# Two fused transformer blocks: the first block's head chain moved two weight blocks forward, function sets loaded by hand, and a normalisation moved into the heads loop

## The reference, cut to what matters

```
f = sigmoid(hf);  g = lb + (1 - lb) * f;  log_g = log(g);  kk = 1 - g
q = silu(hq) * 128 ** -0.5
o = hgrn2_scan(q, kk, hi, log_g)          # decays exp(sums of log_g), pair products, masks
o = rms_norm(o, hg_norm_w) * silu(hg)     # then 16 attention heads, branches, projections
...
uv = gelu(uv); u, v = split(uv)
v = (v - mean(v)) * rsqrt(var(v) + 1e-5) * ln_g + ln_b      # over 1024 channels
y_a = u * (einsum(w_s, v) + b_s)
```

## Time and profile before

| | |
|---|---|
| median of 3 runs | 2972.29 us (2972.26 to 2983.88) |
| profiled execution | 2973.5 us, span of the instructions 2971.7 us |
| PE busy | 2883.4 us, 97% of the span |
| DVE busy | 2171.6 us, 73% |
| ACT busy | 1504.5 us, 51% |
| mean granted TensorE clock | 0.992 |

### The profile page before, as it was taken

How to read it: one execution, slowest core, us unless ns; L and a number is a source line. 1 busy time by engine, 2 the same in 40 slices (tenths; PEclk the granted TensorE clock), 3 DMA queues, 4 the chain that set the end, 5 groups by cost and what they waited for, 6 DMA issues and landing times.

```text
span 2971.7 us, 42894 instructions
## 1 busy us (share of the span) xinstructions
PE 2883.4 (97%) x16334; PEld 2470.7 (83%) x16334; DVE 2171.6 (73%) x3307; ACT 1504.5 (51%) x2256; POOL 123.6 (4%) x121
## 2 busy tenths in 40 slices
PE   8999999999999999999998999999999999999997
PEld 6888888878888888888887888888888888888886
DVE  7777777778777777777786666667768887777775
ACT  5555555556554444444464445455555555555554
POOL 0000000000100000000050000000010000000001
PEclk9999999999999999999999999999999999999999
DMA  6444544445556556556654565555555655555563
GB/s 217 159 157 148 160 148 152 150 137 189 186 185 194 189 189 193 189 187 191 197 172 149 160 180 162 169 180 170 186 181 171 185 191 189 187 185 184 184 191 107
DMA packets 157023, 520.22 MB, mean 175 GB/s; under 512 B 28947, under 2 KB 31379, under 8 KB 156819
## 3 DMA queue, kind: packets, MB, share of 16 engines
q1 hardware_dynamic: 155376, 513.90, 54.2%
q10 hardware_dynamic: 1440, 3.59, 0.3%
HBM read 515.32 MB, written 2.10 MB: 174 GB/s over the span
## 4 chain that ended last, share of the span: by engine, by line
PE 72%; DVE 18%; ACT 6%; issue 4%; DMA 0%; SPq 0%; DVEq 0%; ACTq 0%; POOL 0%; POOLq 0%
PE acc L348 32%; PE acc L350 16%; DVE w_lo L1047 7%; PE psT L348 7%; PE psX L348 7%; ACT w_hi L664 4%; PE psT L350 3%; PE psX L350 3%; DVE work L1053 1%; DVE HS L1190 1%; DVE probs L1121 1%; ACT probs L714 1%; PE acc_first L348 1%; DVE soft L1122 1%; PE psS L476 1%
## 5 line engine op out<-in xcount | busy, mean ns | idle before, releaser
L1047 DVE TENSOR_TENSOR w_lo<-w_raw,w_hi 128x1024 fp32r<-128x1024 f32 (+1 forms) x960 | 1173.9, 1226 | 601.9 <-ACT w_hi L664 590.6
L664 ACT ACTIVATE w_hi<-w_raw 128x1024 fp32r<-128x1024 f32 (+1 forms) x960 | 1004.9, 1053 | 741.7 <-PE acc L350 554.8
L348 PE MATMUL acc<-XU,w_hi 128*128 128x512 f32 x3472 | 1239.1, 400 | 4.5 <-issue 3.9
L350 PE MATMUL acc<-XU,w_lo 128*128 128x256 f32 x3472 | 973.7, 280 | 0.0
L348 PEld LDWEIGHTS acc<-XU,w_hi 128*128 128x128 f32 x3472 | 655.2, 189 | 163.7 <-issue 7.5
L348 PE MATMUL acc<-XY,w_hi 128*128 128x512 f32 x2112 | 757.7, 402 | 13.7 <-DVE G L1053 4.6
L350 PEld LDWEIGHTS acc<-XU,w_lo 128*128 128x128 f32 x3472 | 658.1, 190 | 1.1
L350 PE MATMUL acc<-XY,w_lo 128*128 128x256 f32 x2112 | 592.5, 281 | 0.0
L348 PEld LDWEIGHTS acc<-XY,w_hi 128*128 128x128 f32 x2112 | 398.8, 189 | 118.4 <-issue 8.5
L350 PEld LDWEIGHTS acc<-XY,w_lo 128*128 128x128 f32 x2112 | 400.6, 190 | 0.1
L348 PE MATMUL psT<-XY,w_hi 128*128 128x512 f32 x632 | 225.6, 398 | 5.0 <-DVE w_lo L1047 4.5
(11 more groups left out here) (233 smaller groups left out, 2513.9 us busy)
## 6 DMA issues: line engine op xcount, KB each, us to landing
w_raw<-in_weights SPq DMA_DIRECT2D x956, 512.0 KB, 3.7
bias<-in_rel_bias SPq DMA_DIRECT2D x8, 384.0 KB, 5.6
bias<-in_rpb_back SPq DMA_DIRECT2D x32, 96.0 KB, 6.4
w_raw<-in_weights SPq DMA_DIRECT2D x8, 384.0 KB, 3.1
hT<-in_x_t SPq DMA_DIRECT2D x8, 256.0 KB, 6.1
out_dram<-G ACTq DMA_DIRECT2D x4, 512.0 KB, 3.1
G<-in_range_sums ACTq DMA_DIRECT2D x1, 576.0 KB, 4.6
G<-in_pair_masks ACTq DMA_DIRECT2D x1, 576.0 KB, 5.6
```

What stands on the lines that cost most here:

```text
L348: nc.tensor.matmul(bank[:, :], hi[:, k, col:col + P], X[:, k0 + k, :], start=first and k == 0, stop=False, skip_group_check=True)
L350: done = nc.tensor.matmul(bank[:, 0:T], lo[:, k, col:col + P], X[:, k0 + k, 0:T], start=False, stop=last and k == nk - 1, skip_group_check ...
L664: act.activation(w_hi[s][:, 0:n], w_raw[s][:, 0:n], ACT.Copy).then_inc(hi_done, 1)
L1047: V.tensor_tensor(w_lo[s][:, 0:n], w_raw[s][:, 0:n], w_hi[s][:, 0:n].bitcast(F32), ALU.subtract).then_inc(lo_ready, 1)
```

## The change

1. In `heads1` the tiles hf and hq change places (the weight stream too), and the chain from the sigmoid of hf to the last masks runs two block positions earlier: transposes at b = 5, decays at 6, 8, 10, 12, pair products at 8, 10, 12, 14. `tile_pairs` goes from 18 to 17, `scan_out` from 19 to 18, the head's norm from 21 to 20. The scores, the softmax and the gate tiles stay where they were.
2. Function sets are loaded by hand: the sigmoid set at b = 0, the one with Ln just before it at b = 3 and the sigmoid set again behind it, and at b = 5 a set that holds both Ln and Exp. The same set is loaded ahead of the norms and of the last phase, the sigmoid set ahead of the branches, Gelu and then Ln/Exp in `heads2`.
3. The two norms before `gmv` move behind its second block. The value sums go behind blocks 5, 7, ... 15 of `gmv` and 0 and 1 of `heads2`; centring, squares and their sums into blocks 2 to 6 of the first iteration of `heads2`. There the values are normalised at b = 7 instead of 0, and transposed and mixed behind blocks 7 and 8 instead of 4 and 6.
4. The 16 multiplications of `hT` (L1329) move from `gmv` to two per iteration of `heads2`.

```diff
             after1 = {
-                7: [transpose_pair(wk(0), "lg_ready", "lgT_full")],
-                8: [decays(0)],
+                5: [transpose_pair(wk(0), "lg_ready", "lgT_full")],
+                6: [decays(0)],
+                8: [pair_products(0), decays(1)],
                 9: [transpose_pair(wk(5), "vi_ready", "vT_full")],
-                10: [pair_products(0), decays(1)],
-                12: [pair_products(1), decays(2)],
+                10: [pair_products(1), decays(2)],
+                12: [pair_products(2), decays(3)],
                 13: [scores(0, P, 1)],
-                14: [pair_products(2), decays(3), transpose_pair(wk(5), "avz_ready", "avT_full", "v_ready")],
+                14: [pair_products(3), transpose_pair(wk(5), "avz_ready", "avT_full", "v_ready")],
                 15: [scores(1, T, 1)],
-                16: [pair_products(3)],
-                18: [tile_pairs],
-                19: [scan_out, prob_transposes(0, 1)],
-                20: [attend(0, 1), prob_transposes(1, 1)],
-                21: [scan_rms, attend(1, 1)],
+                17: [tile_pairs],
+                18: [scan_out],
+                19: [prob_transposes(0, 1)],
+                20: [scan_rms, attend(0, 1), prob_transposes(1, 1)],
+                21: [attend(1, 1)],
             }
...
+            first2 = after2 | {
+                0: [value_sums(value_sum, 6)],
+                1: [value_sums(value_sum, 7)],
+                4: [value_sums(value_square_sum, 0, 1, 2, 3)],
+                6: [value_sums(value_square_sum, 4, 5, 6, 7)],
+                7: [scores(0, T, 2), transpose_pair(wk(3), "vh_ready", "vh_full")],
+                8: [mix, transpose_pair(wk(5), "avz_ready2", "avT_full2")],
+            }
...
@@ ACT, heads1 @@
+                    if i and b == 0:
+                        act.preload_act_table(ACT.Sigmoid)
                     if b == (1 if i else 4):
+                        sigmoid_of(0, "hf_z", "hf_sig", i)
+                    if b == (3 if i else 4):
+                        act.wait_ge(S("g_ready"), i + 1)
                         sigmoid_of(2, "hq_z", "hq_sig", i)
-                    if b == (3 if i else 4):
-                        act.wait_ge(S("q_ready"), i + 1)
-                        sigmoid_of(0, "hf_z", "hf_sig", i)
+                        act.preload_act_table(ACT.Ln)
+                        act.activation(wk(0), wk(0), ACT.Ln).then_inc(S("lg_ready"), 1)
+                        act.preload_act_table(ACT.Sigmoid)
                     if b == 5:
-                        act.wait_ge(S("g_ready"), i + 1)
-                        sigmoid_of(3, "hg_z", "hg_sig", i)
-                        act.activation(wk(0), wk(0), ACT.Ln).then_inc(S("lg_ready"), 1)
-                    if b == 7:
                         act.wait_ge(S("lgT_full"), i + 1)
                         act.activation(lg_hi[:, :, :], psT[:, 0:T], ACT.Copy).then_inc(S("lg_hi_ready"), 1)
-                    if b in (8, 10, 12, 14):
-                        k = (b - 8) // 2
+                        act.wait_ge(S("q_ready"), i + 1)
+                        sigmoid_of(3, "hg_z", "hg_sig", i)
+                        act.preload_act_table_set(LOG_EXP)
+                    if b in (6, 8, 10, 12):
+                        k = (b - 6) // 2
...
@@ DVE, first iteration of heads2 @@
+                    if b == (0 if i else 7):
+                        if i == 0:
+                            dve.wait_ge(S("gv_rstd"), 1)
+                        normalized_values(i)
+                    if i == 0 and b == 2:
+                        dve.wait_ge(S("gv_sum"), 1)
+                        link(V.tensor_scalar(wk(8), psT[:, 0:T], 1.0 / WIDTH, None, ALU.mult))
+                    if i == 0 and 2 <= b < 6:
+                        center(2 * b - 4)
+                        center(2 * b - 3)
+                    if b == (6 if i else 9):
+                        mixed_values(i)
```

More of the change, by code:

```diff
@@ L579, in _, with value_sum, value_square_sum @@
             ffn("ffn1last", 0, XY, XU, S("act1_ready"))
+            def value_sum(t):
+                pe.wait_ge(S("gv_ready"), t + 1)
+                done = nc.tensor.matmul(psT[:, 0:T], ones[:, :], G[:, 24 + t, :], start=t == 0, stop=t == HEADS - 1)
+                if t == HEADS - 1:
+                    done.then_inc(S("gv_sum"), 1)
+            def value_square_sum(t):
+                pe.wait_ge(S("gv_sq"), t + 1)
+                nc.tensor.matmul(psE[:, 0:T], ones[:, :], value_squares[t % 4], start=t == 0, stop=t == HEADS - 1)\
+                  .then_inc(S("gv_sq_used"), 1)
             p = ph["gmv"]
@@ L592, in _ @@
                     rms_sum(1, psX)
[L593 to L601, removed]
+                if b % 2 and b >= 5:
+                    value_sum((b - 5) // 2)
             def mix(i):
+                if i == 0:
+                    pe.wait_ge(S("ws_in"), 16)
                 pe.wait_ge(S("vn_ready"), i + 1)
@@ L609, in mix, with value_sums, job @@
                 done.then_inc(S("mix_full"), 1)
+            def value_sums(which, *tiles):
+                def job(i):
+                    for t in tiles:
+                        which(t)
+                return job
             after2 = {
@@ L668, in copy_cross @@
                 act.wait_ge(w_used, p.block(i, b) + 1)
-                act.activation(cross[:, c % 2, :], bank[:, T:2 * T], ACT.Copy).then_inc(cross_ready, 1)
+                act.activation(cross[:, p.cross(i, c) % 2, :], bank[:, T:2 * T], ACT.Copy).then_inc(cross_ready, 1)
             def rstd(dst, src, width, eps, tmp, done):
@@ L884, in _ @@
                         copy_cross(p, i, t, b, acc[t % 2])
+                    if b == 0:
+                        act.preload_act_table(ACT.Gelu_apprx_tanh)
                     if b == 1:
@@ L948, in ffn2 @@
                     tile += s.half if s.kind == "up" else (2 if s.group < 0 else 1)
+            act.preload_act_table(ACT.Silu)
             ffn2("ffn2first", 0)
@@ L1052, in tile_sum @@
                 dve.wait_ge(cross_ready, p.cross(i, c) + 1 - RAW // 2)
-                mark(V.tensor_tensor(dst, bank[:, 0:T], cross[:, c % 2, :], ALU.add), acc_free,
+                mark(V.tensor_tensor(dst, bank[:, 0:T], cross[:, p.cross(i, c) % 2, :], ALU.add), acc_free,
                      p.tile(i, t) + 1 + TILE_CREDIT)
@@ L1191, in _ @@
                              S("qE_ready"), i * 4 + k + 1)
-                    if b == 9:
-                        scaled_tile(p, i, 4, b, 4, bank, wk(7), S("k_z"), i + 1)
-                    if b in (10, 12, 14, 16):
-                        k = (b - 10) // 2
+                    if b == 6:
+                        dve.wait_ge(S("hg_sig"), i + 1)
+                        if i == 0:
+                            dve.wait_ge(S("hgw_in"), 16)
+                        link(V.scalar_tensor_tensor(wk(3), wk(3), hgw, wk(4), ALU.mult, ALU.mult))
+                    if b == 7:
+                        scaled_tile(p, i, 3, b, 3, bank, wk(5), S("vi_ready"), i + 1)
+                    if b in (8, 10, 12, 14):
+                        k = (b - 8) // 2
                         a, h = divmod(k, 2)
@@ L1208, in _ @@
                                 link(ins)
+                    if b == 9:
+                        scaled_tile(p, i, 4, b, 4, bank, wk(7), S("k_z"), i + 1)
+                        dve.wait_ge(S("bias1_in"), 16 * i + 16)
+                        link(V.memset(bias[0:64, :, P:P + 64], MASKED))
                     if b == 11:
@@ new lines, in normalized_values, with mixed_values @@
+            def normalized_values(i):
+                link(V.tensor_tensor(work[:, 3:4, 0:T], G[:, ds(i + 24, 1), :], rsv.rearrange("p (a t) -> p a t", a=1), ALU.mult))
+                mark(V.tensor_scalar(wk(3), wk(3), cols[:, ds(i + C_LNG, 1)], cols[:, ds(i + C_LNB, 1)], ALU.mult, ALU.add),
+                     S("vh_ready"), i + 1)
+            def mixed_values(i):
+                dve.wait_ge(S("mix_full"), i + 1)
+                if i == 0:
+                    dve.wait_ge(S("bs_in"), 32)
+                bs = HS[:, 2:4, :, :].rearrange("p a b c -> p (a b) c")[:, ds(i, 1), :].to_broadcast([P, NT, P])
+                link(V.tensor_tensor(wk(1).rearrange("p (a t) -> p a t", a=NT), psA[:, 0:T].rearrange("p (a t) -> p a t", a=NT),
+                                     bs, ALU.add))
+                dve.wait_ge(S("u_ready"), i + 1)
+                mark(V.tensor_tensor(wk(1), wk(1), wk(0), ALU.mult), S("ya_z2"), i + 1)
+                dve.wait_ge(S("yah_ready2"), i + 1)
+                mark(V.tensor_tensor(XU[:, ds(i, 1), T:2 * T], work[:, 1:2, 0:T],
+                                     XU[:, ds(i, 1), 0:T].bitcast(F32), ALU.subtract), S("ya_ready2"), i + 1)
@@ L1467, in weight_block @@
         t = b // 2
-        starts = [0, 1, 3, 2, 5, 4, 6]
+        starts = [1, 0, 3, 2, 5, 4, 6]
         col = starts[t] * WIDTH + i * P if t < 7 else (7 * WIDTH + (t - 7) // 2 * D + (t - 7) % 2 * P + i * (2 * P))
```

157 lines of the change are left out of this document (77 added, 80 removed).

## The result

| | before | changed |
|---|---|---|
| median, fresh runs (18 each) | 2981.78 us (2970.38 to 2999.74) | 2992.20 us (2981.36 to 3004.71) |
| ratio, 95% interval | | 1.0035 (1.0019 to 1.0051) |
| profiled execution | 2973.5 us, clock 0.992 | 3000.5 us, clock 0.990 |

The change costs 10.4 us (5.7 to 15.2), where +0.4 was forecast.

What follows compares the result with a forecast made beforehand. PE, busy 97% of the span, was taken as the bound, so only its idle time, slow clock or added work counts. The terms summed to +0.4 on 2972.3, rounded 2973 us, own range 2962 to 2984 (chance 0.60).

Steps and rivals of the forecast that it cites:

- `tile_pairs`: First heads: PE's eight waits for DVE's mask products go, -21.6 us.
- `lg_lo` and the transposes ahead of it: First decay in the heads: PE's wait for the logarithm's low part grows from 1.05 to 3.4 us, +18.1 in sum.
- `scan_out`: First heads: a new wait for ACT's copy `AT`, 1.5 us eight times, +12.0 us.
- slow clock in the heads: Slow clock behind all seven `lg_lo` waits of 3.4, none behind those of 1.5: 10.5 instead of 6.0, +4.5 us.
- start of `branch1`: End of the heads: `branch1` waits about 0.6 instead of 3.07 us, without slow clock, -4.0 us.
- `gmv` and `heads2`: Third tile's wait and clock -5.4, sums between stages -7.6, new idles in the first iteration of `heads2` +5.7 us.
- last norm: End of the run: one load less on the path to the output, -1.3 us.
- rival (a): The wait at `scan_out` doesn't come: 12 us less, 2961 us; chance 0.13.
- the idles of 2.7 in the first iteration: First iteration of `heads2`: PE idle 2.3 us behind block 4 and 2.7 behind block 7.
- rival (b): `lg_lo` wait stays 1.05, no wait at `scan_out`, no slow clock in the heads: -40, 2932 us; chance 0.10.
- (d): Each function load in the `lg_lo` chain is followed by 1.38 us idle: 19 more, 2992 us; chance 0.02.
- Rival (c): Wait at `scan_out` is 2.6 us and slows the clock in every head: 21 more, 2994 us; chance 0.13.

Runs made afterwards that it cites:

- heads: Only the first heads' part of the change (chain two blocks forward, hand-loaded function sets, tiles, branch start) put into the kernel before: 2999.03 us, ratio 1.0049.
- sigload: Changed kernel with ACT's second sigmoid load put behind `lg_hi`; ran once, only waits read: 11.4 us less idle time at the first decay.
- lgfirst: Changed kernel with DVE making `lg_lo` before the tile's sum and scaling; ran once, only waits read: 7.0 us less idle time at the first decay.
- lgboth: Changed kernel with the second sigmoid load behind `lg_hi` and `lg_lo` made before the tile: 2969.45 us, ratio 0.9957 against the kernel before.
- before_third: The kernel before, unchanged, executed a third time for one look at the pace: 2972.29 us.
- maskearly: Kernel before with DVE's mask product of the last four pair products ahead of block 16's low part, not behind it: 2954.19 us, ratio 0.9905.
- scan19: Changed kernel with `scan_out` back in block 19, its result's copy and the norm's start behind it: 2964.57 us, ratio 0.9952 against the kernel before.
- all3: Changed kernel with `scan_out` back in block 19, and `lg_lo` without the sigmoid load and the tile ahead of it: 2953.38 us, ratio 0.9907.

## Why the prediction was wrong

The stage sheet against the steps of the forecast (before is the mean of the four executions with its heads, 625.9 us, and of the five with its second heads, 483.9; changed that of the two with its heads, 643.2, and for the second heads that of the eight executions with the gate values' part as in the change, 481.4):

| step | forecast | measured |
|---|---|---|
| `tile_pairs` | -21.6 | -21.6 |
| `lg_lo` and the transposes ahead of it | +18.1 | +17.5 (25.0 + 1.2 - 8.7) |
| `scan_out` | +12.0 | +15.0 |
| slow clock in the heads | +4.5 | +6.3 (24.6 against 18.3) |
| start of `branch1` | -4.0 | -4.5 (2.7 idle, 1.8 clock) |
| `gmv` and `heads2` | -7.3 | -2.5 |
| last norm | -1.3 | -1.3 |
| sum | +0.4 | +8.9, with the whole run +10.4 (5.7 to 15.2) |

The step that failed is the last sentence on `gmv` and `heads2`: "The multiplications of `hT` are off PE's path in both places." They are off it in `gmv`, but at block 10 of the second heads they stand in a stretch in which DVE is already late with the tile sums. That was worth 5 to 6 of the 9 us: with the scaling elsewhere this part gains 8.0, close to the 7.3 forecast. The trace of before that I read has no wait there. The slack would have told: in its second iteration DVE's sum ends at 1711.44, and PE, which needs it, starts at 1711.50.

```profile
1711.02 0.42 DVE L1053 TENSOR_TENSOR work<-acc,cross 128x256 f32<-128x256 f32 x1
```

```profile
1711.50 0.50 PE L348 MATMUL acc<-XY,w_hi 128*128 128x512 f32 x1
```

With 0.06 us to spare, an operation of 0.48 ahead of the sum must show. It showed as 0.54 to 0.94 us in each second head; what is beyond 0.42 is not explained. In the second execution of before three waits of 0.22 stand at this place.

Two terms were mis-sized. `scan_out` waits 1.80 to 2.01, not 1.5: I had granted DVE back the gap of 0.4 in its stretch. And I counted no slow clock behind it, since it came behind 2.7 sometimes and behind 1.05 never, although 1.5 lay between the two and no row covered it; it followed four times in eight. Against that, the mean of before was itself higher than in the one execution that I read (18.3 us, not 14.5).

A reading was wrong too, and it happened not to matter. The prediction calls DVE's stretch up to the second softmax tile "almost without a gap" and uses that against rival (a). One gap of 1.97 stands in it, a wait for ACT's rounding behind the first softmax tile. The added work could have gone into it; it did not, because the change has the same gap at the same place. First before, then changed:

```profile
307.24 1.23 DVE L1047 TENSOR_TENSOR w_lo<-w_raw,w_hi 128x1024 fp32r<-128x1024 f32 x1 [1.97 <-ACT w_hi L664]
```

```profile
319.61 1.23 DVE L1092 TENSOR_TENSOR w_lo<-w_raw,w_hi 128x1024 fp32r<-128x1024 f32 x1 [1.97 <-ACT w_hi L691]
```

Right were the mechanisms and their places: `tile_pairs` freed, `lg_lo` at 3.3 through a load, the roundings and a tile, ACT's copy late behind the softmax at `scan_out`, the idles of 2.7 in the first iteration. Rival (a), no wait at `scan_out`, rival (b), the change as it looks, and (d) are excluded by the rows of waits. Rival (c) had the right place but a wait of 2.6; its clock term came true in half. The absolute level moved as well: before had a median of 2972.29 in three runs and of 2981.78 in eighteen, so 9.5 of the 19.5 us between the forecast 2972.7 and 2992.2 have nothing to do with the change. Of the other 10.0 the terms above explain 8.5, and 1.5 stay open. That rival (c) reads 2994 is therefore luck: it is near only by the level.

## What to carry to other kernels

A chain that is moved earlier by whole blocks brings every link two blocks closer to its producer; work each link anew against the order on its engine, down to the loads and tiles that stand ahead of it. Before moving a chain, look whether the late instruction merely stands behind another that waits: putting it ahead cost 1.9 us of new waits here and saved 21.6. And an operation that is "hidden" must be checked at its new place by the slack there (end of the producer against start of the consumer); a table of waits is silent until the slack is used up.

## What the runs showed of the hardware

**Slow clock behind short idles.** In the 14 profiles of this case I counted PE's idle times by length and how many had over 0.8 us lost to products at the lower clock in the 9 us behind them, or up to the next idle time over 0.9: 0.9 to 1.3 us, 0 of 86; 1.3 to 1.75, 4 of 36; 1.75 to 2.2, 26 of 65; 2.2 to 2.8, 37 of 55; 2.8 to 3.4, 42 of 50. One such event costs 0.9 to 2.9 us, half of them between 1.5 and 1.9. So a wait should be charged with its share: an estimate from these counts is some 0.6 us on top of 2 and 1.1 on top of 2.5. What decides is open, but the events are not independent. Five profiles have both the wait for `lg_lo` and the one at `scan_out` (changed, heads, sigload, lgfirst, lgboth). The latter, 1.8 to 2.1 us, was followed by a slow clock in 13 of the 17 heads that had one behind the first decay, and in 5 of the 23 that had none there. Repairing one wait can so change what a later one costs.

**Two paces at full clock.** A pair of a 512-column and a 256-column product starts every 347 or every 353 ns, and keeps to one of them through nearly a whole feed-forward stage; in the heads, where PE is interrupted every few us, both occur side by side. The first feed-forward stage takes about 716.5 us at the one and about 729.4 at the other, the last 687.4 and 695.8 to 697.6. Of the 14 profiled executions two had both stages at 347 (before_third, maskearly), five both at 353 (the changed kernel, heads, scan19, lgboth, all3), seven one of each. Where the first runs at 353, 13.0 us are lost without any wait in the profile. The times of lgboth fit it: eight lie between 2966.1 and 2972.3, four between 2981.4 and 2983.4. What chooses the pace is open; no run here tried to set it. Nor is it settled whether the kernels differ in how often it is slow: the first stage ran at 353 in five of the seven profiled executions with the moved chain and in one of the seven without. The sheet keeps this out of the account of the change; the fresh times cannot. The two paces are why a single execution of this kernel can't tell 10 us, and why waits and clocks of a stage are the better measure.
